# Prompt attention in a hybrid decoder step: dense tiles first, then sparse ones, with the side work spread one piece per step

## The reference, cut to what matters

```
def block(args):                                   # one tile of 128 prompt rows
    mla_o = mla_attend(ql, qp, qpos, c_kv, k_pe, lw['w_uv'])      # softmax(q k + causal) v
    idx = indexer_topk(qi, wi, qpos, k_i, topk)    # sum over heads of relu(q_i k_i) * w_i, best 132
    dsa_o = dsa_attend(qb, qpos, gather_rows(k_b, idx), gather_rows(v_b, idx), idx)
    return mla_o, dsa_o
...
o = sigmoid(gate_a) * (mla_o @ w_br_a) + sigmoid(gate_b) * (dsa_o @ w_br_b)
x = x + o @ w_o                                    # then the MLP, with a width-3 convolution
```

## Time and profile before

| | us |
|---|---|
| median of three runs | 1731.18 |
| profiled execution | 1730.1 |
| its span | 1728.3 |
| PE busy in the span | 1620.8 (94%) |
| DVE busy | 870.2 (50%) |
| ACT busy | 419.2 (24%) |
| POOL busy | 316.4 (18%) |
| mean granted PE clock | 0.956 of full speed |

### The profile page before, as it was taken

One profiled execution on the slowest core, in us unless ns is written; L12 is line 12 of the kernel. 1 busy time (PEld: TensorE's weight loads), 2 busy tenths in 40 slices (PEclk: granted clock), 3 DMA queues, 4 the chain that ended last, 5 costly groups with the idle time before them and its releaser, 6 DMA issues.

```text
span 1728.3 us, 21560 instructions
## 1 busy us (share of the span) xinstructions
PE 1620.8 (94%) x8540; PEld 985.8 (57%) x8540; DVE 870.2 (50%) x1640; ACT 419.2 (24%) x1112; POOL 316.4 (18%) x332
## 2 busy tenths in 40 slices
PE   5999989999999799998878899999999999989998
PEld 3654455446776465665455566447777777744443
DVE  3447799999993878774773343222322323210011
ACT  2131312001004455553446531001111111100010
POOL 2100000010004757760446730000000000000000
PEclk8899998999999899997779999999999999999999
DMA  6521203142406778767446845312122122111100
GB/s 191 187 75 62 89 30 128 64 180 93 150 36 226 254 273 328 288 239 217 114 131 185 310 121 196 103 37 72 49 79 68 49 74 73 49 61 49 66 23 32
DMA packets 87541, 218.36 MB, mean 126 GB/s; under 512 B 13320, under 2 KB 37264, under 8 KB 83440
## 3 DMA queue, kind: packets, MB, share of 16 engines
q0 software_dynamic: 26864, 116.66, 19.8%
q1 hardware_dynamic: 60578, 100.33, 17.7%
HBM read 199.99 MB, written 16.84 MB: 125 GB/s over the span
## 4 chain that ended last, share of the span: by engine, by line
PE 82%; DVE 9%; DMA 3%; POOL 2%; issue 2%; ACT 2%; DVEq 0%; SPq 0%; ACTq 0%
PE PS L2186 13%; PE PS L647 13%; PE PS L2231 11%; PE PS L2214 7%; PE PS L698 7%; PE PS L2163 4%; PE PS L766 3%; PE PS L1116 2%; PE PS L1050 2%; PE PS L1704 2%; POOL mem L1943 2%; PE PS L2140 2%; PE PS L1584 2%; PE PS L2603 1%; PE PS L1686 1%
## 5 line engine op out<-in xcount | busy, mean ns | idle before, releaser
L647 PE MATMUL PS<-mem 128*128 128x512 f32 (+3 forms) x580 | 232.7, 557 | 0.0
L2186 PE MATMUL PS<-mem 128*128 128x376 f32 x704 | 231.7, 481 | 0.0
L2231 PE MATMUL PS<-mem 128*128 128x512 f32 (+1 forms) x440 | 190.7, 595 | 1.4 <-DVE mem L2410 1.4
L2186 PEld LDWEIGHTS PS<-mem 128*128 128x128 f32 x704 | 131.0, 189 | 79.3
L647 PEld LDWEIGHTS PS<-mem 128*128 128x128 f32 (+1 forms) x580 | 99.8, 185 | 119.1 <-issue 118.9
L1943 POOL DMA_INDIRECT mem<-in_cache_dsa_k,mem x128 | 136.8, 1069 | 147.2 <-issue 135.5
L1943 POOL DMA_INDIRECT mem<-in_cache_dsa_v,mem x128 | 123.3, 964 | 143.4 <-PE PS L1686 107.5
L2231 PEld LDWEIGHTS PS<-mem 128*128 128x128 f32 (+1 forms) x440 | 80.1, 182 | 111.4 <-issue 109.8
L2214 PE MATMUL PS<-mem 128*128 128x216 f32 x704 | 135.8, 345 | 0.0
L2214 PEld LDWEIGHTS PS<-mem 128*128 128x128 f32 x704 | 129.2, 189 | 10.7
L2391 DVE TENSOR_SCALAR mem<-mem 128x528 f32<-128x528 f32 x22 | 12.2, 555 | 238.7 <-ACT mem L2294 238.7
(11 more groups left out here) (332 smaller groups left out, 2033.0 us busy)
## 6 DMA issues: line engine op xcount, KB each, us to landing
mem<-in_w_in SPq DMA_DIRECT2D x10, 2048.0 KB, 8.2
mem<-in_w_ffn_g SPq DMA_DIRECT2D x11, 1024.0 KB, 5.3
mem<-in_w_ffn_u SPq DMA_DIRECT2D x11, 1024.0 KB, 5.3
mem<-in_w_ffn_d SPq DMA_DIRECT2D x10, 1024.0 KB, 5.0
tmp_gates<-mem SPq DMA_DIRECT2D x16, 296.0 KB, 2.1
mem<-tmp_gates SPq DMA_DIRECT2D x16, 296.0 KB, 3.7
mem<-in_w_o SPq DMA_DIRECT2D x2, 2048.0 KB, 10.6
mem<-in_x_prompt SPq DMA_DIRECT2D x6, 512.0 KB, 12.3
```

The costliest lines, as they stand in the source:

```text
L647: ins = pe.matmul(PS[0:n, b[bank], out_at:out_at + width], left[:, k, cols], w[:, k, at:at + width], start=k == 0, stop=k == k_range - 1)
L2186: pe.matmul(PS[:, 3 * (f % 2) + j, 0:UP_A], w[:, k, :], h2T[:, k, 0:UP_A], start=k == 0, stop=k == KD - 1)
L2231: return pe.matmul(PS[0:TW[m], (5 * n + m) % 8, :], upT[:, f, token_cols(m)], w[:, i, :], start=f == 0, stop=f == NF - 1)
```

## The change

The order of the steps becomes a4, a0, a1, a2, a3, b4, b0, b1, b2, b3. The side work is put on other steps: one index pair per step in steps 0 to 3 and 10 to 13 (before two per step in 0, 1, 6 and 7); the picks of tile 2 over six steps (4 to 9) and of tile 3 over eight (14 to 21), before over four each; the value rows nearly evenly over steps 0 to 27, with three more after that and none in the last four steps; one branch product per step over steps 20 to 35, before two per step over 28 to 35. Both quads of kind a use banks 6 and 7, and the first value row no longer waits for the mask of the second quad.

```
-        pairs_p = (tile("a", 4, quads) + tile("a", 0) + tile("b", 4, quads) + tile("a", 1) + tile("b", 0, range(2)) +
-                   tile("a", 2) + tile("b", 0, range(2, 4)) + tile("a", 3) + tile("b", 1) + tile("b", 2) + tile("b", 3))
+        pairs_p = (tile("a", 4, quads) + tile("a", 0) + tile("a", 1) + tile("a", 2) + tile("a", 3) +
+                   tile("b", 4, quads) + tile("b", 0) + tile("b", 1) + tile("b", 2) + tile("b", 3))
...
-        pick_at = {pair_no["a", host, i]: (m, i) for host, m in ((0, 2), (1, 3)) for i in range(4)}
...
-        late = pair_no["b", 1, 0]
+        pick_at = {n: (2, n - 4, 6) for n in range(4, 10)} | {n: (3, n - 14, 8) for n in range(14, 22)}
+        v_cost = [{("b", 2): 2, ("b", 3): 0}.get(x[0:2], 7) for x in pairs_p]
+        late = pair_no["b", 0, 0]
...
-        parts_at = {late + 4 + n: parts[2 * n:2 * n + 2] for n in range(8)}
+        parts_at = {late + n: parts[n:n + 1] for n in range(16)}
...
+        index_at = {n: [("i", 2, n)] for n in range(4)} | {n: [("i", 3, n - 10)] for n in range(10, 14)}
...
-            if n in parts_at:
-                pe_order.append(("part", parts_at[n][1]))
...
-                banks_p[g] = [0, 1] if g == ("a", 4, 1) else [6, 7]
+                banks_p[g] = [6, 7]
...
-                if q == 0:
-                    pe.wait_ge(sem("masked"), upto("masked", ("a", 4, 1)))
...
-            def pick(m, h):
+            def pick(m, part, parts):
...
-                for _ in range(rounds * h // H, rounds * (h + 1) // H):
+                for _ in range(rounds * part // parts, rounds * (part + 1) // parts):
...
-                if n in parts_at:
-                    mix_part(parts_at[n][1])
```

More of the change, by code:

```diff
@@ L1497, in trunk @@
         stat_p = {g: stat[:, 2 * (pair_no[x] % 3) + j, :] for x in pairs_p for j, g in enumerate(heads_of(x))}
-        pick_at = {pair_no["a", host, i]: (m, i) for host, m in ((0, 2), (1, 3)) for i in range(4)}
-        v_cost = [{("a", 4): 0, ("b", 4): 4, ("a", 0): 6, ("b", 0): 3, ("a", 1): 6, ("b", 1): 5, ("a", 2): 7,
-                   ("b", 2): 4, ("a", 3): 8, ("b", 3): 5}[x[0:2]] for x in pairs_p]
-        late = pair_no["b", 1, 0]
+        pick_at = {n: (2, n - 4, 6) for n in range(4, 10)} | {n: (3, n - 14, 8) for n in range(14, 22)}
+        v_cost = [{("b", 2): 2, ("b", 3): 0}.get(x[0:2], 7) for x in pairs_p]
+        late = pair_no["b", 0, 0]
         parts = [(ft, c) for ft in range(KD) for c in range(2)]
-        parts_at = {late + 4 + n: parts[2 * n:2 * n + 2] for n in range(8)}
+        parts_at = {late + n: parts[n:n + 1] for n in range(16)}
         part_cols = [slice(0, UP_A), slice(UP_A, NCOL)]
@@ L1861, in pick @@
                 all_s = score_acc[:, 0:4 + keys]
-                for _ in range(rounds * h // H, rounds * (h + 1) // H):
+                for _ in range(rounds * part // parts, rounds * (part + 1) // parts):
                     link(dve.max(top8_p, all_s))
                     link(dve.match_replace(all_s, top8_p, all_s, TAKEN))
-                if h == H - 1:
+                if part == parts - 1:
                     mask = mask_of[m]
@@ L1886, in dve_prompt @@
                 if n in pick_at:
-                    m, i = pick_at[n]
-                    pick(m, 2 * i)
+                    m, i, steps = pick_at[n]
+                    pick(m, 2 * i, 2 * steps)
                 for i in index_at.get(n, []):
@@ L1895, in dve_prompt @@
                     invert(g)
-                if n in parts_at:
-                    mix_part(parts_at[n][1])
                 if n in pick_at:
-                    m, i = pick_at[n]
-                    pick(m, 2 * i + 1)
+                    m, i, steps = pick_at[n]
+                    pick(m, 2 * i + 1, 2 * steps)
             dve.wait_ge(sem("o_new_out"), upto("o_new_out"))
```

## The result

The changed kernel takes 1702.01 us in the median (1700.04 to 1706.72, four executions), beside 1730.47 us of the kernel before on the same chip: a ratio of 0.984, with a 95% interval from 0.9819 to 0.9861. A second set of runs gave 1699.19 us, 0.9806 (0.9787 to 0.9826). The forecast was 1707 us, with a range from 1693 to 1729.

The account below looks back on a forecast made before the run. PE's work was taken as badly spread from first quad to branch b's projection: starved early by DVE and ACT chains, then by gathers, overfull last. Step groups summed to 220.0 us instead of 243.8, giving 1707 us, range 1693 to 1729.

Parts of the forecast that it names:

- The bound: From first quad to branch b's projection, 243.8 us: a shift of its end carries one to one to the end.
- the section: PE's timeline from the first quad to branch b's projection, 243.8 us before, forecast 220.0 us.
- The sum: New length of PE's stretch from first quad to branch b's projection, added by step groups: 220.0 us, 23.8 less than 243.8.
- steps 0 to 3: Two quads, two a0 steps, four index pairs, eight rows: 7.5 us each, 30 in all, bounds 24 and 38.
- 4 to 9: Steps with the picks of tile 2, paced by DVE: 32 us, bounds 28 and 40.
- The in-step waits: PE waiting for ACT's copy of four rows: covered by branch products, DVE's picks or allowances; 9.0 us over five places before.
- The eight places: Steps 5, 7, 9, 16, 18, 20, 25, 27, where a row opens a new group behind one that closes a group.
- Rival 1: Early chains in steps 10 to 13 (+5.5 us) and ACT copy waits (+7) cost more than allowed: 1719 us, chance 0.20.
- Rival 2: POOL's gathers pace steps 10 to 27 and PE's 9.0 us of waits for them return: 1716 us, chance 0.12.
- The cover: Steps 10 to 27: POOL's gathers supply 40 rows in 100 us, PE uses them in 110; called thin.
- Rival 3: PE stays at the lower clock through steps 0 to 13, 115 us instead of 86.5: slower, 1736 us, chance 0.10.
- What would show it: Signs in the new trace, such as PE idle below 20 us, first branch product near 932, last eight steps 5.2 each.

Follow-up runs that it names:

- rows later: The changed kernel with two value rows in each of steps 4 to 35 and none in the first four; 1692.18 us, 0.9773 of the kernel before.
- index paired: The changed kernel with two index pairs per step again, in steps 0, 1, 10 and 11; 1696.32 us, 0.9789 of the kernel before.
- rows aligned: The changed kernel with two value rows in each of steps 0 to 31, so groups of four end with a step; 1685.30 us.
- copy first: The changed kernel with ACT's copy of a finished row group put ahead of the step's exponentials; 1698.85 us, 0.9811 of the kernel before.
- products paired: The changed kernel with two branch products per step over steps 28 to 35, as before; 1716.70 us, 0.9901 of the kernel before.

## Why the prediction was right, and where it was off

- **The bound.** It held: over all traces, whose front has the same instructions, the section begins between 809.83 and 815.92 us, and the tail behind it moved by 1.4 us; the whole gain is in the section. That the profiled execution came to 1706.72 us, beside the 1706.3 of my sum, is luck: the section was 6.1 us shorter than I summed, and this execution happened to reach it 5.1 us late.
- **The sum.** 213.94 us instead of 220.0. By groups, measured and forecast: steps 0 to 3 22.75 (30), 4 to 9 33.50 (32), 10 to 13 22.60 (24.5), 14 to 17 23.99 (24), 18 to 19 12.35 (11), 20 to 21 16.26 (17.5), 22 to 27 35.22 (33), 28 to 31 19.64 (20.5), 32 to 35 21.38 (21), tail 6.25 (6.5).
- **The mis-sized term** is steps 0 to 3, 7.25 us shorter, and below the lower bound of 24. I took the 8.02 us of the first step, with two pairs, as the start for all four, and left out what the other steps of that kind take in the trace before: there the two a0 steps take 4.9 us each, and the four steps together, with the same index pairs and four rows, take 24.72 us, from 810.81 to the scores of step 4:

```profile
835.53 0.61 PE L1584 MATMUL PS<-mem 96*128 96x128 f32 x4
```

Nor did the chain through ACT and DVE set a time of 7.5 us a step: it is 22.75 us with eight rows, 21.72 without any (rows later) and 23.2 with the pairs doubled (index paired). The remaining groups differ by +1.2 in sum.

- **The in-step waits.** The eight places were right, the claim that they are covered was wrong. The products in steps 20, 25 and 27 shorten them to 1.08 us, about what ACT's two small copies take by themselves (0.35 and 0.58 us in step 20); the picks in 5, 7 and 9 do not cover them at all, because they are part of the chain that the copy waits for. Steps 4 to 9 came near my 32 us by luck: with the same picks rows aligned takes 23.62 us there, below my lower bound of 28, and DVE's last three rounds run on into step 10. So 28 us were too many for DVE's pace, and the copy waits made up the difference. What the claim would have been worth is at most the 16 us of section of rows aligned, which has the slower rows too.
- **Rival 1** was right in this half (I had put four waits of 1.8 us there, and there were eight of 1.08 to 2.94), and wrong in its other: index pairs in steps 10 to 13 cost 22.60 us, not 30.
- **Rival 2**, the gathers. PE has no wait for them in the change, and the last gather begins at 979.32 us (1028.02 before). The cover was as thin as I wrote: with the copies moved ahead, 10.1 us of such waits appear.
- **Rival 3**, the lower clock. The first 100 us ran at 0.89 and not near 0.5. The Trainium skill's page "TensorE: Matmul & The Clock Gate", section "HAM oscillation — how this bites in real kernels", on which I leaned for it, lets the clock fall in bursts that alternate with waits. The trace agrees for steps 4 to 9, at 0.64, 0.79 and 0.57 behind three waits, but no such stretch of the change lasts long. In the early steps, with idle stretches of at most 1.00 us, the clock was 0.88.
- **What would show it.** PE idle 20.8 us (said below 20), first branch product at 931.53 us without a wait (said 932), the last eight steps (1023.61 - 982.59) / 8 = 5.13 us each (said 5.2).

## What to carry to other kernels

Where side work shares a buffer in groups, let a group end where a step of the main work ends: a hand-over in the middle of a step waits for everything that the other engine has queued ahead of its small copy. A wait is not hidden by work that is itself a part of the chain that one waits for, so before calling a wait covered, follow the releasing engine's stream back to what it waits for itself. Price a step from every step of that kind in the trace, not from the first. And when a wait is taken away, look at once at the next slowest supplier, here the gathers, and give it the slack as well.

## What the runs showed of the hardware

PE's clock was low behind shorter idle stretches than I had read from the kernel before, where 3.34 and 3.04 us stood ahead of slow work: idle stretches of 2.47, 2.94 and 2.94 us are followed by stretches at a mean of 0.64, 0.79 and 0.57, and the first row behind the one of 2.47 us took 1.04 us. Behind the two of 2.94 us the first row took 0.62 us, so the fall comes a little later there. An idle stretch of nearly this length does not always bring it: in copy first 2.35 us, ended at 848.74 us, are followed by 6 us at a mean of 1.00. In rows aligned PE is idle 3.95 us over steps 4 to 9, in pieces of at most 0.85 us, at a mean clock of 1.00. And work without a gap did not always end it soon: in products paired PE was busy for all of 23.07 us at 0.50.
